# Constant matmuls in TensorE's waits, and an inverse transform with its frequency loop outermost

## What is computed

```python
def first_block(...):                       # two layers
    h = rms_norm(x, norm_mix[layer])
    x = x + s5_mixer(h, ...)                # layer 0
    x = x + stick_breaking_attention(h, w_q, k_shared, v_shared, w_o)   # layer 1
    x = x + conv_ffn(rms_norm(x, norm_ffn[layer]), ...)   # both, F = 2816
    kv = rms_norm(x, norm_kv) @ kv_w        # after layer 0
    return rms_norm(x, norm_final)
# attention, one block of queries
log_beta = log_sigmoid(z)
log_one_minus = where(causal, log_beta - z, 0.0)
rem = cumsum(log_one_minus, axis=3, reverse=True) - log_one_minus
w = where(causal, exp(log_beta + rem), 0.0)
# second_block: an attention mixer, then the Hyena mixer
kern = kern / sum(abs(kern), axis=0, keepdims=True)
k_f = rfft(kern, axis=0)
for o in range(2):
    z = parts[o + 1] * (irfft(rfft(z, n=2 * L) * k_f[o], n=2 * L)[:L] + z * skip[o])
return (z * silu(gate)) @ w_out             # then a last rms norm
```

## Time and profile before

| what | value |
|---|---|
| median of 3 runs | 2302.84 us (2299.04 to 2306.05) |
| the profiled execution | 2304.46 us |
| its span | 2302.7 us |
| mean granted clock of TensorE | 0.962 |
| TensorE (PE) busy | 2166.6 us |
| DVE busy | 1256.4 us |
| ACT busy | 746.9 us |
| POOL busy | 686.1 us |

### The profile page before, as it was taken

One profiled execution on the slowest core, in us unless ns is written; L12 is line 12 of the kernel. 1 busy time (PEld: TensorE's weight loads), 2 busy tenths in 40 slices (PEclk: granted clock), 3 DMA queues, 4 the chain that ended last, 5 costly groups with the idle time before them and its releaser, 6 DMA issues. The chain is left out here.

```text
span 2302.7 us, 27418 instructions
## 1 busy us (share of the span) xinstructions
PE 2166.6 (94%) x10821; PEld 1585.2 (69%) x10821; DVE 1256.4 (55%) x2284; ACT 746.9 (32%) x1067; POOL 686.1 (30%) x408
## 2 busy tenths in 40 slices
PE   7859899999999998999999999999999999998988
PEld 6848688888878766778888855436874437885653
DVE  8562389984352066278882032358763563225862
ACT  3422332222142366233232131325651232332210
POOL 6614244445444300344444410011000342441000
PEclk9979899999989999999999989998999979999999
DMA  4032244444423200234443320120002213222102
GB/s 178 7 55 84 72 140 149 141 124 130 131 74 100 83 1 1 82 110 145 148 137 92 92 116 24 55 73 21 2 2 92 92 73 129 92 92 92 74 19 73
DMA packets 51535, 195.49 MB, mean 85 GB/s; under 512 B 9417, under 2 KB 9593, under 8 KB 46191
## 3 DMA queue, kind: packets, MB, share of 16 engines
q1 hardware_dynamic: 37440, 148.53, 20.3%
q0 software_dynamic: 10240, 44.04, 5.5%
q10 hardware_dynamic: 3728, 1.18, 0.3%
HBM read 179.04 MB, written 10.49 MB: 82 GB/s over the span
## 5 line engine op out<-in xcount | busy, mean ns | idle before, releaser
L1474 POOL TENSOR_TENSOR w_lo<-raw,w_hi 128x1024 fp32r<-128x1024 f32 (+1 forms) x216 | 513.7, 2379 | 879.3 <-ACT w_hi L1111 879.2
L586 PE MATMUL psum<-h_hi,w_hi 128*128 128x512 f32 x1216 | 487.9, 401 | 7.7 <-ACT h_hi L1118 5.9
L587 PE MATMUL psum<-h_hi,w_lo 128*128 128x512 f32 x1216 | 480.0, 395 | 0.0
L1111 ACT ACTIVATE w_hi<-raw 128x1024 fp32r<-128x1024 f32 (+1 forms) x216 | 224.9, 1042 | 609.7 <-PE psum L591 399.2
L591 PE MATMUL psum<-h_lo,w_hi 128*128 128x512 f32 x1216 | 303.0, 392 | 0.0
L586 PEld LDWEIGHTS psum<-h_hi,w_hi 128*128 128x128 f32 x1216 | 231.1, 190 | 71.4 <-ACT h_hi L1118 14.4
L591 PEld LDWEIGHTS psum<-h_lo,w_hi 128*128 128x128 f32 x1216 | 230.5, 190 | 48.2
L587 PEld LDWEIGHTS psum<-h_hi,w_lo 128*128 128x128 f32 x1216 | 232.0, 191 | 45.9 <-issue 0.2
L455 PE MATMUL psum<-big,ring 128*128 128x512 f32 x480 | 209.0, 594 | 0.0
L455 PEld LDWEIGHTS psum<-big,ring 128*128 128x128 f32 x480 | 91.0, 191 | 113.8 <-issue 112.7
L633 PE MATMUL psum<-f_hi,w_hi 128*128 128x512 f32 x352 | 137.7, 391 | 0.0
(11 more groups left out here) (374 smaller groups left out, 3326.1 us busy)
## 6 DMA issues: line engine op xcount, KB each, us to landing
raw<-in_ffn_w_up SPq DMA_DIRECT2D x88, 512.0 KB, 3.6
raw<-in_ffn_w_down SPq DMA_DIRECT2D x32, 512.0 KB, 3.6
raw<-in_hy_in SPq DMA_DIRECT2D x32, 512.0 KB, 3.5
ffn_buf<-in_ada_w POOLq DMA_DIRECT2D x20, 512.0 KB, 5.0
sq<-in_ada_w POOLq DMA_DIRECT2D x20, 512.0 KB, 5.0
raw<-in_ssm_w_glu SPq DMA_DIRECT2D x16, 512.0 KB, 3.6
spec<-big SPq DMA_DIRECT2D x8, 1024.0 KB, 3.8
big<-spec POOLq DMA_DIRECT2D x8, 1024.0 KB, 5.1
```

Source lines behind the costliest of these rows:

```text
L586: pe.matmul(o, hi[:, k, :], h_of(k), start=k == 0, stop=False)
L587: pe.matmul(o, lo[:, k, :], h_of(k), start=False, stop=False)
L1111: act.activation(w_hi[:, (n % 2) * HALF:(n % 2) * HALF + w], raw[:, (n % 4) * HALF:(n % 4) * HALF + w], ACT.Copy).then_inc(S["w_hi"], 1)
L1474: pool.tensor_tensor(w_lo[:, at:at + w], raw[:, (n % 4) * HALF:(n % 4) * HALF + w], w_hi[:, at:at + w].bitcast(F32), ALU.subtract).then_in ...
```

## The change

There are three parts. First, a function `keep_clock(n)` on TensorE: it waits for the release of the bank that is to be taken next (or of a named one), and writes n matmuls of the identity with 256 columns of constants into it. The tile that takes the bank next overwrites them. They stand, with n in brackets, before the norm's matmuls of ffn0 (8) and nw0 (3), before the spreads of ffn0 (3), kv (4), ffn1 (4), final, nw0 and final2 (3 each), before the first tile of both ffn up projections and of the key projection (3 each), before scores(0) (3) and cumulate(0) (5) into bank 7, before filter_norm(0) (7), filter_norm(2) (5) and the spectra of u=3 (5), between z_back(0, 0) and z_turn(1, 0) (8), and in the middle of z_back(1, 1) (10): 84 in all. Second, `z_back` on TensorE takes all four banks first and runs over the frequency outermost, so that its first half needs one `yw` less. Third, on DVE the last step, u=7, is done in two halves of 256 columns, each with its fold, products and sums, and z_fold(7) comes after the sums of u=6 rather than before them.

```diff
@@ -408,9 +408,17 @@
...
 
+            def keep_clock(n, bank=None):
+                b = turn[0] % 8 if bank is None else bank
+                if n and last_release[b]:
+                    pe.wait_ge(*last_release[b])
+                for _ in range(n):
+                    pe.matmul(psum[:, b, 0:256], mat("ident"), mats[:, 0:256], start=True, stop=True)
+
...
                 src, n, m, _ = norm_src(name)
+                keep_clock({"ffn0": 8, "nw0": 3}.get(name, 0))
...
@@ -431,6 +439,7 @@
...
                 key, r, n = ("rb", name), R_RELEASE.get(name), norm_src(name)[1]
+                keep_clock({"ffn0": 3, "kv": 4, "ffn1": 4, "final": 3, "nw0": 3, "final2": 3}.get(name, 0))
...
@@ -573,9 +582,10 @@
...
 
-            def lin_split(key_of, w, tiles, hi_wait, lo_wait, beside=None, x_base=None, h=None):
+            def lin_split(key_of, w, tiles, hi_wait, lo_wait, beside=None, x_base=None, h=None, keep=0):
...
 
+                keep_clock(keep)
...
@@ -619,7 +629,8 @@
...
                         ada_turn(ADA_UP1 * l + t // 2 - 1)
-                lin_split(lambda t: (f"up{l}", t), A[f"ffn_w_up{l}"], 2 * FT, h_hi_wait(f"ffn{l}"), h_lo_wait(f"ffn{l}"), beside)
+                lin_split(lambda t: (f"up{l}", t), A[f"ffn_w_up{l}"], 2 * FT, h_hi_wait(f"ffn{l}"), h_lo_wait(f"ffn{l}"), beside,
+                          keep=3)
...
@@ -644,7 +655,7 @@
...
             norm("kv")
-            lin_split(lambda t: ("k", t), A["kv_k"], 8, h_hi_wait("kv"), h_lo_wait("kv"))
+            lin_split(lambda t: ("k", t), A["kv_k"], 8, h_hi_wait("kv"), h_lo_wait("kv"), keep=3)
...
@@ -674,6 +685,7 @@
...
                 if h == 0:
+                    keep_clock(3, 7)
...
@@ -688,6 +700,7 @@
...
                 if h == 0:
+                    keep_clock(5, 7)
...
@@ -921,6 +934,7 @@
...
                 key = ("nrm", u)
+                keep_clock({0: 7, 2: 5}.get(u, 0))
...
@@ -946,6 +960,8 @@
...
                         key = ("fs", u, f, a)
+                        if (u, f, a) == (3, 0, 0):
+                            keep_clock(5)
...
@@ -987,19 +1003,23 @@
                     fills(i, key)
 
             def z_back(o_, hf):
-                for c in range(4):
-                    key = ("y", o_, 4 * hf + c)
-                    o = take(pe, key)
-                    if c == 0:
-
-                        pe.wait_ge(S["yw"], 2 * (2 * o_ + hf + 1))
-                    for par in range(2):
-                        for f in range(2):
+                keys = [("y", o_, 4 * hf + c) for c in range(4)]
+                for f in range(2):
+                    for c in range(4):
+                        if f == 0:
+                            take(pe, keys[c])
+                        elif (o_, hf, c) == (1, 1, 0):
+                            keep_clock(10)
+                        o = ps(keys[c])
+                        if c == 0 or (o_, hf, f, c) == (1, 1, 1, 2):
+                            pe.wait_ge(S["yw"], 2 * (2 * o_ + hf) + f + 1 + c // 2)
+                        for par in range(2):
                             for q, tab in enumerate((INVC, INVS)):
                                 i = pe.matmul(o[:, par * 256:par * 256 + 256], YW[hf][:, f, 2 * q + par, c * P:(c + 1) * P],
-                                              tab[:, f, par * 256:par * 256 + 256], start=f == 0 and q == 0,
-                                              stop=f == 1 and q == 1)
-                    fills(i, key)
+                                              tab[:, f, par * 256:par * 256 + 256], start=f == 0 and q == 0 and par == 0,
+                                              stop=f == 1 and q == 1, skip_group_check=True)
+                        if f:
+                            fills(i, keys[c])
 
 
             z_turn(0, 0)
@@ -1009,6 +1029,7 @@
...
             z_back(0, 0)
+            keep_clock(8)
...
@@ -2147,42 +2168,54 @@
             for t in range(8):
                 dve.wait_ge(*free(("z0", t)))
                 dve.sem_inc(S["z_ready"], 1)
-            def z_fold(u):
+            def z_fold(u, n=slice(0, 512)):
 
                 ks = [("sp", u, a) for a in range(4)]
-                if u >= 2:
+                if u >= 2 and n.start == 0:
                     dve.wait_ge(S["yw"], u - 1)
                 for a in range(4):
                     dve.wait_ge(*full(ks[a]))
                 dve.wait_ge(*free(ks[1]))
                 dve.wait_ge(*free(ks[3]))
-                cs, oc, os_ = CS[u % 2], OCS[:, 0, :], OCS[:, 1, :]
-                TT(cs[:, 0, 0:512], ps(ks[0]), oc, ALU.add).then_inc(S["cs_ready"], 1)
-                frees(TT(cs[:, 0, 512:1024], ps(ks[0]), oc, ALU.subtract), ks[0])
-                TT(cs[:, 1, 0:512], ps(ks[2]), os_, ALU.add).then_inc(S["cs_ready"], 1)
-                frees(TT(cs[:, 1, 512:1024], os_, ps(ks[2]), ALU.subtract), ks[2])
-
-            def z_products(u):
-
-                C, Sn = CS[u % 2][:, 0, :], CS[u % 2][:, 1, :]
-                Kr, Qi = SPEC[u % 2][:, 0:1024], SPEC[u % 2][:, 1024:2048]
-                dve.wait_ge(S["cs_ready"], 2 * (u + 1))
-                dve.wait_ge(*free(("sp", u, 0)))
-                dve.wait_ge(*free(("sp", u, 2)))
+                cs, oc, os_ = CS[u % 2].rearrange("p a (s n) -> p a s n", s=2), OCS[:, 0, n], OCS[:, 1, n]
+                last = n.stop == 512
+                for i, (k, ops) in enumerate(((ks[0], ((oc, ALU.add), (oc, ALU.subtract))),
+                                              (ks[2], ((os_, ALU.add), (os_, None))))):
+                    TT(cs[:, i, 0, n], ps(k)[:, n], ops[0][0], ALU.add).then_inc(S["cs_ready"], 1)
+                    x, y = (ps(k)[:, n], ops[1][0]) if ops[1][1] else (ops[1][0], ps(k)[:, n])
+                    j = TT(cs[:, i, 1, n], x, y, ALU.subtract)
+                    if last:
+                        frees(j, k)
+                    else:
+                        step(j)
+
+            def z_products(u, n=slice(0, 512)):
...
-                dve.wait_ge(S["cs_ready"], 2 * (u + 1))
+                dve.wait_ge(S["cs_ready"], 2 * (u + 1) + 2 * (u == 7 and n.start > 0))
@@ -2219,11 +2252,14 @@
...
                     z_fold(5)
-                after = z_products(u)
-                if u not in (4, 7):
-                    if u != 3:
+                parts = [slice(0, 512)] if u < 7 else [slice(0, 256), slice(256, 512)]
+                for n in parts:
+                    if u == 7:
+                        z_fold(u, n)
+                    after = z_products(u, n)
+                    if u not in (3, 4, 6, 7):
                         z_fold(u + 1)
-                z_sums(u, after)
+                    z_sums(u, after, n)
...
```

More of the change, by code:

```diff
@@ new lines, in z_products @@
+            def z_products(u, n=slice(0, 512)):
+                C, Sn = (CS[u % 2][:, i, :].rearrange("p (s n) -> p s n", s=2)[:, :, n] for i in range(2))
+                Kr, Qi = (SPEC[u % 2][:, i * 1024:(i + 1) * 1024].rearrange("p (s n) -> p s n", s=2)[:, :, n]
+                          for i in range(2))
+                pr, pq = (PD[:, i * 1024:(i + 1) * 1024].rearrange("p (s n) -> p s n", s=2)[:, :, n] for i in range(2))
+                dve.wait_ge(S["cs_ready"], 2 * (u + 1) + 2 * (u == 7 and n.start > 0))
+                if n.stop == 512:
+                    dve.wait_ge(*free(("sp", u, 0)))
+                    dve.wait_ge(*free(("sp", u, 2)))
+                else:
+                    own()
@@ L2172, in z_products @@
                 dve.wait_ge(S[f"spec_in{u % 2}"], 16 * (u // 2 + 1))
-                step(TT(PD[:, 0:1024], C, Kr, ALU.mult))
-                step(TT(PD[:, 1024:2048], Sn, Qi, ALU.mult))
+                step(TT(pr, C, Kr, ALU.mult))
+                step(TT(pq, Sn, Qi, ALU.mult))
                 real = steps[0]
@@ L2178, in z_products, with z_sums @@
                 return real, steps[0]
-            def z_sums(u, after):
+            def z_sums(u, after, n=slice(0, 512)):
                 hf, f = (u // 2) % 2, u % 2
-                C, Sn = CS[u % 2][:, 0, :], CS[u % 2][:, 1, :]
+                C, Sn = (CS[u % 2][:, i, :].rearrange("p (s n) -> p s n", s=2)[:, :, n] for i in range(2))
+                pr, pq = (PD[:, i * 1024:(i + 1) * 1024].rearrange("p (s n) -> p s n", s=2)[:, :, n] for i in range(2))
                 dve.wait_ge(S["dve_step"], after[0])
-                step(TT(PD[:, 0:1024], PD[:, 0:1024], PD[:, 1024:2048], ALU.subtract))
+                step(TT(pr, pr, pq, ALU.subtract))
                 real = steps[0]
@@ L2192, in z_sums @@
                 dve.wait_ge(S["dve_step"], real)
-                step(TT(YW[hf][:, f, 0, :], PD[:, 0:512], PD[:, 512:1024], ALU.add))
-                step(TT(YW[hf][:, f, 1, :], PD[:, 0:512], PD[:, 512:1024], ALU.subtract))
+                step(TT(YW[hf][:, f, 0, n], pr[:, 0], pr[:, 1], ALU.add))
+                step(TT(YW[hf][:, f, 1, n], pr[:, 0], pr[:, 1], ALU.subtract))
                 dve.wait_ge(S["dve_step"], imag)
```

(4 more changed lines are left out.)

## The result

The changed kernel takes 2309.3 us (median of 15 runs, 2304.65 to 2310.89) against 2303.55 for the kernel before (15 runs), a ratio of 1.0025 with a 95% interval of 1.0017 to 1.0033. That is 5.8 us slower, where the sum gave 5.15 us faster; against the forecast of 2298.5 with its range of 2288 to 2308 it lies 1.3 us above the range. The two profiled executions differ by less, 2306.05 to 2304.46, since the changed kernel's is one of its faster runs.

What follows compares the result with a forecast made beforehand. TensorE, busy 94% of the span, bounds the kernel. Norms and attention -6.45, filters +2.6, convolution -1.3 sum to -5.15: 2299.3 from the profiled execution, 2297.7 from the median, middle 2298.5 us; own range 2293 to 2304, with rivals 2288 to 2308.

Steps and rivals of the forecast that it cites:

- Attention, -3.05: From cumulate(0) to ACT's exponential 5.49 us becomes 3.06 (-2.4), and the next head's period 8.53 becomes 7.88 (-0.65).
- Norms, -3.6 and +0.2: Spreads at full clock: ffn0 -0.9, kv -0.9, final and nw0 -1.8; three lo phases together 8.64 us for 8.45, +0.2.
- Filters, +2.6: Fillers behind bank releases at filter_norm(0) and (2) cost +3.1 and +2.2; earlier clock rise -1.0, low stretch at u=3 -1.7.
- Convolution, -1.3: Inverse transform's last half ends at 2232.05 instead of 2233.34; without the ten fillers it would be -5.7.
- z_back(0,0)'s early start: Costed at nothing with its 8 fillers, since TensorE waits for DVE afterwards; +3.5 if that cover went.
- the 4.4 that I gave them: The ten fillers in z_back(1,1) wait for y(1,0)'s bank, drained after u=7, so they cost +4.4 us on the path.
- the reordered end: End of the convolution with frequency outermost and u=7 halved: -5.7 without the ten fillers, including -0.65 from z_back(0,1).
- The fixed cost of an instruction: The halving adds 14 DVE instructions: 0.9 us by the rows, some 2.2 by the page, putting the convolution at about 0.
- rival 1: The clock holds through the hi phases too: lo phases -2.5, filters 1.3 more back, 2294.7 us; chance 0.16.
- Rival 2: Late fillers cost nothing, as bank releases precede the real work's inputs: 5.3 and 4.4 come off, 2288.8 us; chance 0.13.
- Rival 3: Constant matmuls don't hold the clock; fillers take 0.79 us, near 2323 if everywhere, midpoint 2311; chance 0.11.
- My slower case: Measured time above 2309.7 us, chance 0.11, made of most of Rival 3 and a rest.

## Why the prediction was wrong

By part, norms and attention were forecast at -6.45 and measured at -2.7, the filters at +2.6 and +8.2, the convolution at -1.3 and +2.7. The traces of the twelve runs and of the two kernels, one for each, also show what each stage takes when nothing in it is changed. The table is worked out from their timelines: I took the start of the same ACT or DVE instruction in each trace and in the kernel before's, and the growth of the difference over a stage (from and to, by before's times). A minus is shorter than in before's trace. The last row ends with ACT's last instruction. At the filters the run without the late fillers, which keeps the five before the spectra of u=3, is in neither column of others (-2.5).

| stage | others, unchanged there: mean (range), n | the changed kernel | others with the edit, mean, n |
|---|---|---|---|
| norm ffn0, 250 to 290 | -1.4 (-2.0 to -1.1), 9 | -2.2 | -1.6, 3 |
| norm kv, 640 to 680 | +1.2 (0.0 to +1.6), 9 | +0.9 | +1.3, 3 |
| attention, 800 to 830 | -1.7 (-2.0 to +0.4), 8 | -3.2 | -2.9, 4 |
| norm ffn1, 960 to 1000 | +0.2 (-0.1 to +0.6), 9 | +0.5 | +0.6, 3 |
| final and nw0, 1330 to 1376 | -0.1 (-1.5 to +0.1), 9 | -2.7 | -1.7, 3 |
| second attention, 1500 to 1600 | +0.3 (0.0 to +2.6), 9 | 0.0 | +1.6, 3 |
| filters, 1800 to 1925 | -1.4 (-3.4 to +0.1), 7 | +6.2 | +6.3, 1 |
| 2190 to 2292 | -0.9 (-1.4 to -0.1), 5 | +0.6 | +0.4, 1 |

The second column is the lesson: the trace I read from was itself 1.4 to 1.7 us long at ffn0, at the attention and at the filters, and 1.2 short at kv, because its low stretches happened to fall there: at the attention its granted clock is 0.50 for 10.2 us (798.86 to 809.10), in seven of the eight others without an edit there for 3.4 us.

- **Attention, -3.05: wrong in size.** The gain is -1.2. I took 5.49 and 8.53 us from the one trace; in the run with the convolution's edits and fillers, unchanged here, the same way takes 801.58 to 806.29, 4.71, and the next head 7.32:

```profile
801.58 0.41 PE L701 MATMUL psum<-f_lo,tail 128*128 128x384 f32 x1 [2.58 <-DVE f_lo L1940]
```

and ACT's exponentials in the same run:

```profile
806.29 1.24 ACT L1274 ACTIVATE big<-psum 128x1280 f32<-128x1280 f32 x1 [3.49 <-PE psum L720]
...
813.61 1.24 ACT L1274 ACTIVATE big<-psum 128x1280 f32<-128x1280 f32 x1 [0.63 <-PE psum L720]
```

- **Norms, -3.6 and +0.2: half right.** The spreads shrank by 0.9 against before's trace as said. By the table, with the changed kernel among those with the edit, final and nw0 gave -1.8, ffn0 -0.4, kv nothing and ffn1 +0.4. At ffn0 there was little to win: six of the nine kernels without fillers there have the spread at 1.13 too. At kv, wherever the spread is at full clock, with fillers or without, the hi phase takes 9.9 us instead of 9.27, so 0.6 of the 0.9 is lost again there. And the 2.06 of kv's lo phase in the earlier trace rows was the exception: eight of nine kernels without fillers there have 3.0 to 3.6, the four with them 3.2 to 3.6. At ffn1 the lo phase of those four takes 3.1 to 3.6, the mean of the others is 3.0. Three of the four are also 1.6 us longer in the second attention, where nothing was edited, and one kernel without them is 2.6 longer. The traces of these four kernels, and no other, have a low stretch of 3.4 us near 1537 that before's has not (mean granted clock 0.89 against 1.00 from 1530 to 1545); what puts it there stays open. Together with the attention, -6.45 was forecast and -2.7 measured.
- **Filters, +2.6: the place was right and the price wrong, the step that failed most.** Measured +8.2 alone, and +7.6 by the table. I took 0.44 us a filler at a place with 3.25 us of idle in front of it; that idle had cooled the clock, so they took 0.76, 9.3 us for twelve instead of 5.3. I credited -1.0 for the clock's rise: the norm and the spectra of u=0 did save 2.3, but TensorE then idled 3.05 for DVE instead of 1.64 and 0.9 was left. And I credited -1.7 for a low stretch before the spectra of u=3. Of the seven other traces without fillers at the filters four did not have it, so in about half of them there was nothing to win. In the changed kernel the five stood in the gap at full clock, but 2.19 us of idle were left behind them, since DVE was late by the fillers ahead, and the spectra were partly cold again (window 1903 to 1906: 0.55).
- **Convolution, -1.3: wrong sign, by two terms.** I cost z_back(0,0)'s early start at nothing. It moved the 4 us of idle to in front of the transposition, and what is cold there is on the path: about +1.2 in five traces and +0.96 in the changed kernel's. From 2190 on, two traces without the ten fillers are 3.8 and 4.0 us shorter than before's, two with them 0.4 and 0.6 longer, so the ten cost the 4.4 that I gave them. But five unchanged there are 0.9 shorter too, and the cold half took 10.23 where I had 9.1; so of the -5.1 for the reordered end (-5.7 less the -0.65 counted at z_back(0,1)) 3.1 were left. The forecast of what gates it, the fold's banks and not the sums, was right, and undoing that took this part from -4.3 to -7.9.
- **The fixed cost of an instruction.** In the halved step 128x512 products lie 0.60 apart and 256-wide folds 0.33, as in the rows; in the run with the new order and no fillers one half takes 6.95 us (2201.72 to 2208.67) where I had 6.85. The larger estimate by the Trainium skill ("VectorE: DVE Perf Modes", the section on the TRN2 errata), 1.3 us more for the two halves, did not appear.

```profile
2201.72 0.42 DVE L2165 TENSOR_TENSOR scr<-psum,sq 128x256 f32<-128x256 f32 x1 [0.44 <-DVEq L2213]
...
2208.67 0.42 DVE L2165 TENSOR_TENSOR scr<-psum,sq 128x256 f32<-128x256 f32 x1 [0.41 <-DVE ring L2211]
```

- **Rivals.** The clock held through the first steps of ffn0's hi phase (0.50 us an L596 to 276.4) and fell then, so rival 1 fell. Rival 2 is refuted by the 11.5 us between the two places at the filters and by the 7.0 us between the two runs of the convolution. Rival 3 is refuted as a mechanism: fillers let into a gap kept the clock at 1.00 nearly everywhere. They ran cold where it was low already: behind the waits at the filters, and in six more groups without a wait directly in front, where TensorE had worked with gaps. These are the three at nw0 in three traces (2.6 to 2.9 us, 1.56 at full clock) and the five one tile ahead of filter_norm(2) in three (3.9 to 4.1 us, 2.32 at full clock). My slower case had the wrong mechanism; the right one was in the forecast, undersized.

## What to carry to other kernels

A filler that waits for a bank waits for whoever drains it: before placing one, name the bank's last occupant, and if its drain is what ends the idle, put the filler one tile earlier, or leave it out. Price work behind an idle gap at the low clock. And where the clock's low stretches are the thing bought, one trace tells where they fell in one run: compare the same stage in several traces, of any kernels that share it, before writing down a gain of a microsecond or two.

## What the runs showed of the hardware

Matmuls of constants with the identity hold TensorE's clock at 1.00 through gaps of up to 5 us (22 instructions in 4.91 us and a z_back of 14.08 behind them, for 5.07 us of idle and 16.9 to 17.1), so here they count as work. They don't lift it at once where it has fallen: seven of them began at the low level after 3.33 us of idle and their window shows 0.57, and three at nw0, in the run with the fillers of norms and attention alone, behind matmuls with 0.23 us of idle between them, took 2.82 us at a granted clock of 0.51, for 1.56 at 1.00. The places of the low stretches differ from trace to trace also in stages where the kernels are the same, and with them the times of these stages: at the filters seven kernels without an edit there are spread over 3.5 us, in the second attention nine over 2.6.
